# Where the operands of TensorE's products lie in SBUF, modulo 256 bytes

## The reference

```python
h = rmsnorm(x, norm_g[i, 0]); proj = h @ w_in[i]    # 9216 columns, split in seven parts
y_a = rg_lru(conv(rnn_in)) * gelu(rnn_gate); y_b = diff_attention(q, k, v)
merged = sigmoid(g_a) * (y_a @ w_proj_a[i]) + sigmoid(g_b) * (y_b @ w_proj_b[i])
x = x + rmsnorm(merged @ w_out[i], norm_g[i, 1])
h = rmsnorm(x, norm_g[i, 2])
f = swiglu(h, ffn_w_gate, ffn_w_up, ffn_w_down)    # layer 0, inner width 3584
f = sum over top-2 of 8 experts of combine * swiglu(h, w_gate[e], w_up[e], w_down[e])   # layer 1
x = x + rmsnorm(f, norm_g[i, 3])
gate = sigmoid(rmsnorm(x, norm_g[i, 4]) @ ple_w_gate[i])
x = x + rmsnorm(gate * (p[i] @ ple_w_proj[i]), norm_g[i, 5])
```

## Time and profile before

| | before |
|---|---|
| median of 3 runs | 1839.1 us (1839.0 to 1843.63) |
| profiled execution | 1839.69 us |
| its span, first to last instruction | 1838.0 us |
| TensorE busy | 1794.3 us, 98% |
| VectorE busy | 1490.0 us, 81% |
| ScalarE busy | 1302.3 us, 71% |
| read from HBM and written | 503.87 MB and 7.88 MB, 278 GB/s over the span |

### The profile page before, as it was taken

The page is one execution under the profiler, slowest core; times in us unless marked ns, Lnnn a source line. Parts: engine busy times, 40 slices in busy tenths (PEclk is TensorE's granted clock), DMA queues, the critical chain, the costliest instruction groups (busy, mean ns, idle before and its releaser), DMA issues.

```text
span 1838.0 us, 29753 instructions
## 1 busy us (share of the span) xinstructions
PE 1794.3 (98%) x10521; PEld 1568.4 (85%) x10521; DVE 1490.0 (81%) x1948; ACT 1302.3 (71%) x1726; POOL 112.3 (6%) x138
## 2 busy tenths in 40 slices
PE   6999999999999999999999999999999999999997
PEld 6998999999879999977888888888888888888785
DVE  7887667666468886668989989989899898998996
ACT  6757547454477657467878888788887887888776
POOL 1200000000010200002000000010000100000300
PEclk8999999999999999999999999999999999999999
DMA  9663555565545744567999999999999999999991
GB/s 308 206 186 124 174 195 185 187 203 194 197 146 174 221 151 140 197 191 254 396 378 380 376 373 387 368 384 366 382 387 370 381 385 369 384 372 374 390 370 49
DMA packets 276048, 517.01 MB, mean 281 GB/s; under 512 B 10754, under 2 KB 114052, under 8 KB 275972
## 3 DMA queue, kind: packets, MB, share of 16 engines
q1 hardware_dynamic: 268400, 493.81, 75.8%
q0 software_dynamic: 7248, 22.06, 3.7%
q10 hardware_dynamic: 324, 0.12, 0.0%
HBM read 503.87 MB, written 7.88 MB: 278 GB/s over the span
## 4 chain that ended last, share of the span: by engine, by line
PE 86%; DVE 6%; ACT 6%; issue 1%; DMA 0%; DVEq 0%; SPq 0%; ACTq 0%
PE bank L1759 81%; DVE wlo L1106 3%; ACT whi L647 1%; PE bank L2216 1%; PE bank L1914 1%; ACT SC L823 1%; ACT SQJ L658 1%; DVE RIN L1213 1%; DVE SC L1241 1%; ACT SC L818 0%; DVE X L1166 0%; PE bank L1870 0%; ACT HH L705 0%; PE bank L2226 0%; PE bank L1797 0%
## 5 line engine op out<-in xcount | busy, mean ns | idle before, releaser
L1106 DVE TENSOR_TENSOR wlo<-raw,whi 128x1024 fp32r<-128x1024 f32 x880 | 1031.6, 1223 | 157.6 <-ACT whi L647 153.8
L647 ACT ACTIVATE whi<-raw 128x1024 fp32r<-128x1024 f32 x880 | 919.4, 1059 | 317.7 <-PE bank L1759 308.9
L1759 PE MATMUL bank<-HH,whi 128*128 128x256 f32 x1296 | 364.5, 281 | 0.0
L1759 PE MATMUL bank<-HL,whi 128*128 128x256 f32 x1296 | 360.6, 278 | 0.0
L1759 PE MATMUL bank<-HH,wlo 128*128 128x256 f32 x1296 | 360.6, 278 | 0.0
L1759 PE MATMUL bank<-whi,XGH 128*128 128x512 f32 x896 | 358.1, 400 | 2.0 <-DVE wlo L1106 1.9
L1759 PE MATMUL bank<-whi,XGL 128*128 128x512 f32 x896 | 352.0, 393 | 0.0
L1759 PE MATMUL bank<-wlo,XGH 128*128 128x512 f32 x896 | 348.6, 389 | 0.0
L1759 PEld LDWEIGHTS bank<-HH,wlo 128*128 128x128 f32 x1296 | 244.8, 189 | 0.0
L1759 PEld LDWEIGHTS bank<-HH,whi 128*128 128x128 f32 x1296 | 243.6, 188 | 0.9 <-issue 0.7
L1759 PEld LDWEIGHTS bank<-HL,whi 128*128 128x128 f32 x1296 | 244.1, 188 | 0.2
(11 more groups left out here) (349 smaller groups left out, 2083.8 us busy)
## 6 DMA issues: line engine op xcount, KB each, us to landing
raw<-in_moe_w_gate_dram SPq DMA_DIRECT2D x112, 1024.0 KB, 7.1
raw<-in_moe_w_up_dram SPq DMA_DIRECT2D x112, 1024.0 KB, 7.6
raw<-in_moe_w_down_dram SPq DMA_DIRECT2D x112, 1024.0 KB, 6.0
raw<-in_w_in_dram SPq DMA_DIRECT2D x56, 1024.0 KB, 5.8
raw<-in_ffn_w_gate_dram SPq DMA_DIRECT2D x14, 1024.0 KB, 5.1
raw<-in_ffn_w_up_dram SPq DMA_DIRECT2D x14, 1024.0 KB, 5.0
raw<-in_ffn_w_down_dram SPq DMA_DIRECT2D x14, 1024.0 KB, 5.0
raw<-in_w_proj_a_dram SPq DMA_DIRECT2D x8, 1024.0 KB, 5.1
```

Source lines behind the costliest of these rows:

```text
L647: nc.scalar.activation(whi[b % SPL][:, r], raw[b % RAW][:, r], ACT.Copy).then_inc(s_hi, 1)
L1106: v.tensor_tensor(wlo[b % SPL][:, r], raw[b % RAW][:, r], whi[b % SPL][:, r].bitcast(F32), ALU.subtract).then_inc(s_lo, 1)
L1759: ins = mm(dst, a, b, start=start and n == 0, stop=stop and n == 2, skip_group_check=True)
```

## The change

The instructions are the same, in the same order and with the same waits on all five engines; their addresses change. SGN, of which only the first column was ever used, is cut from 128 columns to one, which frees 480 bytes. A helper `beside(off, phase)` rounds an offset up to the next one that lies `phase` bytes behind the first weight slot, modulo 256 (`LANE`). `arena` is rounded to 192 (`MOVING`), and `a1`, 16 KB behind it, to 0 (`HELD`). The block diagonal tile BD lies 8 KB + 256 behind `o_rin` rather than 8 KB + 128, and YAL and all later tiles of the mixer's part with it. The dense layer's second tiles (FH, FL, FS, FA) and the experts' (XGH, XGL, ATH, ATL, MS) are counted from `a1`.

```diff
+LANE = 256
+MOVING, HELD = 192, 0
...
         raw = [keep(f"raw{i}", [P, CH]) for i in range(RAW)]
+        first = cursor[0]
         whi = [keep(f"whi{i}", [P, CH], F32R) for i in range(SPL)]
...
-        SGN = keep("SGN", [P, P])
+        SGN = keep("SGN", [P, 1])
...
-        arena = cursor[0]
+
+        def beside(off, phase):
+
+            return off + (first + phase - off) % LANE
+
+        arena = beside(cursor[0], MOVING)
...
         o_rin = a0 + 16 * KB
+        a1 = beside(o_rin, HELD)
         RIN = at("RIN", o_rin, [P, KT, SEQ + 3])
-        o_bd = o_rin + 8 * KB + 128
+        o_bd = o_rin + 8 * KB + LANE
         BD = at("BD", o_bd, [P, 2, KT, P])
         YAH = at("YAH", o_rin, [P, KT, SEQ], F32R)
         YAL = at("YAL", o_bd, [P, KT, SEQ], F32R)
...
-        FH = at("FH", a0 + 16 * KB, [P, FT, SEQ], F32R)
-        FL = at("FL", a0 + 44 * KB, [P, FT, SEQ], F32R)
-        FS = at("FS", a0 + 72 * KB, [P, 2, 512])
-        FA = at("FA", a0 + 76 * KB, [P, 2, 512])
+        FH = at("FH", a1, [P, FT, SEQ], F32R)
+        FL = at("FL", a1 + 28 * KB, [P, FT, SEQ], F32R)
+        FS = at("FS", a1 + 56 * KB, [P, 2, 512])
+        FA = at("FA", a1 + 60 * KB, [P, 2, 512])
...
-        XGH = at("XGH", a0 + 16 * KB, [P, KT, TOKENS], F32R)
-        XGL = at("XGL", a0 + 20 * KB, [P, KT, TOKENS], F32R)
-        ATH = at("ATH", a0 + 24 * KB, [P, FT, TOKENS], F32R)
-        ATL = at("ATL", a0 + 38 * KB, [P, FT, TOKENS], F32R)
+        XGH = at("XGH", a1, [P, KT, TOKENS], F32R)
+        XGL = at("XGL", a1 + 4 * KB, [P, KT, TOKENS], F32R)
+        ATH = at("ATH", a1 + 8 * KB, [P, FT, TOKENS], F32R)
+        ATL = at("ATL", a1 + 22 * KB, [P, FT, TOKENS], F32R)
...
-        MS = at("MS", a0 + 52 * KB, [P, 2, 512])
+        MS = at("MS", a1 + 36 * KB, [P, 2, 512])
```

More of the change, by code:

```diff
@@ L161, in bass_hybrid_rglru_diffattn_moe @@
         PLO = at("PLO", o_rt + 14 * KB, [P, PKT, SEQ], F32R)
-        GROW = (at("GROW0", o_q, [P, D]), at("GROW1", a0 + 72 * KB, [P, D]), at("GROW2", o_q + 8 * KB, [P, D]),
+        GROW = (at("GROW0", o_q, [P, D]), at("GROW1", a1 + 56 * KB, [P, D]), at("GROW2", o_q + 8 * KB, [P, D]),
                 at("GROW3", o_q, [P, D]), at("GROW4", a0 + 12 * KB, [P, D]), at("GROW5", o_q + 8 * KB, [P, D]))
-        ZG = (at("ZG0", o_q + 4 * KB, [P, D]), at("ZG1", a0 + 76 * KB, [P, D]), at("ZG2", o_q + 12 * KB, [P, D]),
+        ZG = (at("ZG0", o_q + 4 * KB, [P, D]), at("ZG1", a1 + 60 * KB, [P, D]), at("ZG2", o_q + 12 * KB, [P, D]),
               at("ZG3", o_q + 4 * KB, [P, D]), at("ZG4", a0 + 52 * KB, [P, D]), at("ZG5", o_q + 12 * KB, [P, D]))
@@ L204, in bass_hybrid_rglru_diffattn_moe @@
         PLACE = at("PLACE", o_l + 512, [P, 5, BLK, EXPERTS])
-        assert a0 + 56 * KB <= o_q
+        assert a1 + 40 * KB <= o_q
         PT = at("PT", o_rt, [P, DEPTH * BLK, PLE])
@@ L491, in _ @@
             pool.memset(IDENT[:, :], 0.0).then_inc(s_pool, 1)
-            pool.memset(SGN[:, 0:1], 1.0).then_inc(s_sgn, 1)
+            pool.memset(SGN[:, :], 1.0).then_inc(s_sgn, 1)
             pool.memset(ONES[:, :], 1.0).then_inc(s_pool, 1)
@@ L508, in _ @@
                 pool.wait_ge(s_sgn, n + 1)
-                pool.affine_select(out=SGN[:, 0:1], in_=SGN[:, 0:1], compare_op=ALU.is_ge, fill=fill, base=-row,
+                pool.affine_select(out=SGN[:, :], in_=SGN[:, :], compare_op=ALU.is_ge, fill=fill, base=-row,
                                    pattern=[[0, 1]], channel_multiplier=1).then_inc(s_sgn, 1)
```

## The result

The changed kernel takes 1829.74 us (median of 6 runs, 1829.12 to 1831.46); the kernel before, run beside it, takes 1841.13 (6 runs, 1837.74 to 1843.63). The ratio is 0.9939, with a 95% interval of 0.9926 to 0.9952: faster by 0.6%. Predicted were 1817 us, within 1785 to 1842. The sign held, and so did the mechanism, that placement alone changes TensorE's step; of the 22 us forecast about half came. The six runs of the kernel before lie in two groups (1837.7 to 1839.1 and 1843.2 to 1843.6), so the difference of the medians, 11.4 us, can be anything from 9 to 14 us by the interval. The stages are compared in the two profiled executions. The profiled execution took 1829.26 us, its span 1827.6 against 1838.0, so 10.4 us are to be placed.

What follows compares the result with a forecast made beforehand. TensorE, busy in 98% of the 1838.0 us span, was taken as the bound, so time is matmuls times step. Terms of -19.2 and -2.8 made -22 us, from 1839.7 to 1817.7, said as 1817 us, range 1785 to 1842.

Steps and rivals of the forecast that it cites:

- YAH, YAL, PHI, PLO: Projections and embedding: with YAL, PHI, PLO moved from 64 to 192, steps fall by about 4.4 ns; sum -2.8 us.
- The fear that the first projection would fall into the higher level: First projection might step like the five mixer chunks at 117.8 ns, leaving -1.1 us instead of -2.8.
- HH, HL at nothing: Mixer and dense chunks: placement stays at 192, so no change entered; level shifts could cost 6 us or give 10.
- XGH to FL: Experts and dense down: 4368 matmuls with held operand moved from 192 to 0, 228.9 to 224.5 ns each, -19.2 us.
- f32 row: Comparison step for 512-column products: 228.9 and 233.3 ns were said to carry surcharge over it, so something was left to lose.
- Rival 1: Experts and dense down: two levels fall, to 1797 us, or three up to VectorE's cap, to about 1788; chance 0.23.
- What would hide a gain: Experts: VectorE caps the gain at 44 us, and transfers need 383 GB/s; a limit there would take 17.7 us.
- More than one level: Experts and dense down: the step falls by two levels (1797 us) or three (about 1788 us); chance 0.23.
- Held distance doesn't matter: Products with held state: the moving operand's place alone decides, leaving 0 to -3 us, 1836 us; chance 0.24, shared with a DMA limit.
- DMAs cap the experts: Experts: landings grow late from 377 GB/s on, leaving 0 to -3 us, 1836 us; chance 0.24, shared with held distance not mattering.
- Its remark that levels also come from elsewhere: Support for held distance not mattering: HH shows two levels at one placement, so levels can come from elsewhere; chance 0.24.
- Distance 0 collides: Experts and dense down: both operands' reads meet at once, step rises to 233.3 ns, +19.2 - 2.8, 1856 us; chance 0.19.

Runs made afterwards that it cites:

- e1: Changed kernel with the held tiles (FH, FL, XGH, XGL, ATH, ATL) back at distance 192, low parts still moved: 1835.46 us, ratio 0.9976 to the kernel before.
- e2: Changed kernel with YAL, PHI, PLO and all tiles behind BD back at 64, held tiles still at 0: 1829.56 us, ratio 0.9943 to the kernel before.
- e3: Changed kernel with HELD at 64 instead of 0: 1854.93 us, ratio 1.0077 to the kernel before.
- e5: Changed kernel with the tiles behind BD and YAL (T2 to SGA, MA, PHI, PLO) back at 64, YAL at 192: 1830.72 us, ratio 0.995 to the kernel before.
- m3: TensorE alone, no part of the reference: six placements, each entered twelve ways behind transposes or f32 products; moving at 192 gave 113.3 ns in 9 entries, 117.8 in 3.
- m1: TensorE alone, no part of the reference: the changed kernel's products with state tiles at eight distances and more; steps 226.7 to 234.2 ns held, 113.3 to 120.0 moving.
- e7: Changed kernel with the mixers' low weights at distance 128 instead of 0, except in the V chunks: 1825.02 us, ratio 0.9923 to the kernel before.
- m2: TensorE alone, no part of the reference: low parts of state and weights each at 0, 64, 128 or 192; state held at 0 gave 226.7 to 233.5 ns.
- e4: Changed kernel with MOVING at 0 instead of 192, so every arena tile is at 0: 1846.81 us, ratio 1.0034 to the kernel before.

## Why the prediction was half right

*YAH, YAL, PHI, PLO: right.* Predicted -2.8 us; the products priced give about 2.5 (1.18 and 1.16 in the projections' stages, some 0.15 for PHI and PLO). That the stages add up to 2.8 is chance in its last 0.3: 0.34 of the 0.38 us in the second embedding's stage lies in the gathering of the first expert's tokens (5.73 to 5.39 us), which the prediction doesn't price. First projection 21.76 us (21.8 predicted), output projection's 48 in 10.98 (10.99). e1 and e2 show that this is the place of YAL and the tiles behind it: it comes with them alone and goes with them. The fear that the first projection would fall into the higher level did not come true: with YAL at 192 the projections' stage is 67.3 us in both layers of the changed kernel, e1, e3 and e5.

*HH, HL at nothing: right, but for 1 us.* Chunks changed level in both directions, 44 of 86 low before and 49 after, which is 1.0 us in the two mixers; dense gate and up didn't move. The open question "what chooses between 113.3 and 117.8" has its answer in m3: both are steady states of one placement, and what runs just ahead chooses. The address of HH itself has no part at the distances tried (m1, 256 and 448). e7 shows it the other way round: with the low weights at 128 the choice is gone where the weights are held.

*XGH to FL: this step failed, by its size.* It said: "I take one level down, 228.9 - 4.4 = 224.5 ns", with "one level is the smallest amount in which steps have moved" as a reason. The 4.4 ns between the mixer's chunks and the dense ones are the distance of two states of one placement (m3), and no size of what a placement gives. Nor are the steps a ladder of 4.4 ns: m1 has 226.7, 228.9, 233.3 and 234.2 on the held side, 113.3, 116.7, 117.3, 117.8, 118.3 and 120.0 on the moving side. What distance 0 gives is 2.2 ns, 4368 x 2.2 = 9.7 us instead of 19.2. That the step would fall at all was not derived either: no row had both operands at 0, and m1's 233.3 at most other distances shows how near the other side was. So the sign of this term was in part luck.

No run shows the 224.5 ns: the lowest step at 512 columns is 226.7 (m1, m2, m3). Nor does one show that the "f32 row", with which the same sentence compares, is a measure for it. That row is 215.4 ns, (1.89 - 0.382)/7 from the earlier trace rows, and it is the step of one record: the 32 f32 products of U and BD that the kernel issues have 64 records, and the 120 of 256 columns in m3 (L97) have 240. Such a product takes two steps, 431 ns, where an fp32r product of 256 columns takes 113.3. That one of these records is the work of 512 fp32r columns was the author's estimate. Rival 1's 13.5 ns for the dense matmuls, behind the 1788 us of the range, are 228.9 less these 215.4, and no run shows them either: 2.2 ns came. The 215 and 108 ns of the rivals in m1 and m2 stand near the same row and its half; 226.7 and 113.3 are the lowest steps there.

*What was left out: the settling.* Of those 9.7 us, about 6.5 arrived: 0.62 in dense down's 288 matmuls, 8 times 0.74 in the experts. (The stages give 1.27 and 5.19, the same sum by chance: 0.65 of it lies behind dense down, in work that the change doesn't price, and the last expert's gate and up took 0.31 us more than before rather than less, with TensorE's waits for `wlo` there at 1.0 us instead of 0.6.) TensorE's timeline of the changed kernel in the fourth expert, behind transposes of MA:

```profile
1322.16 0.60 PE L2225 MATMUL bank<-IDENT,MA 128*128 128x128 f32 x4
1322.52 0.48 PE L1768 MATMUL bank<-whi,XGH 128*128 128x512 f32 x1
1322.83 0.40 PE L1768 MATMUL bank<-wlo,XGH 128*128 128x512 f32 x1
...
1324.46 0.40 PE L1768 MATMUL bank<-whi,XGL 128*128 128x512 f32 x1
```

and at the same place in the kernel before:

```profile
1330.67 0.60 PE L2216 MATMUL bank<-IDENT,MA 128*128 128x128 f32 x4
1331.03 0.48 PE L1759 MATMUL bank<-whi,XGH 128*128 128x512 f32 x1
...
1332.95 0.39 PE L1759 MATMUL bank<-whi,XGL 128*128 128x512 f32 x1
```

Eight steps take 1.94 us after (1322.52 to 1324.46) and 1.92 before, though the steady step is shorter after. An expert has nine such interruptions, seven by MA and two by XROW. The first 16 steps behind MA's take 3761 ns (median) in both kernels, so the 35 ns that 16 shorter steps should give are missing. From behind one interruption to behind the next, 48 products and 4 transposes, after and before:

```profile
1107.80:1119.18 11.38, 11.38 (x55) 9.40 (x54) 10.37 (x11) 9.36 (x11) 0.00 (x0) 1.00 1.05 387
1114.97:1126.42 11.45, 11.45 (x55) 9.41 (x54) 10.37 (x11) 9.35 (x11) 0.00 (x0) 1.00 1.05 387
```

That is 0.07 us less, where 48 x 2.2 ns are 0.11. So each interruption takes back 0.04 us, nine of them 0.37: 504 x 2.2 = 1.11 less 0.37 is 0.74, as measured. Over eight experts that is 3.0 us, and 9.7 - 3.0 = 6.7. m3 shows the same sign with TensorE alone. The rows before held a hint: two experts take 238.95 us between equal starts, 0.45 more than the 238.5 added up from steady steps and transposes.

*What would hide a gain: right that it doesn't.* In the changed kernel's experts two to seven TensorE keeps to its steps, with VectorE at 90%; only in the first and the last expert does it wait for `wlo`, 0.6 and 1.0 us in all (1.4 and 0.6 before).

*The rivals.* More than one level: fell, no placement of m1 or m2 at 512 columns is under 226.7 ns. Held distance doesn't matter: fell by e3 and m1. DMAs cap the experts: fell by the changed kernel's own, which run at 226.7 ns with 380 GB/s. Its remark that levels also come from elsewhere was true: one placement can have two. Distance 0 collides: fell for the products of 512 columns that it was about. But those of 256 columns stand at 120.0 ns there, the highest level of m1's row, with the state moving or held (e4, m2). The 233.3 ns that this rival named are a real step too: e3 runs near it, and m1 has 234.2 at distance 96.

*Open.* Why these distances act as they do. The best are 0 at 512 columns and 192 at 256, and the low parts count too (m2); no rule was found that gives both. Why MA's place alters its transposes and the products behind them (118.74 against 118.51) was seen, not explained.

## What to carry to other kernels

Where TensorE is busy all the time, read its step from start times, and if equal products have unequal steps, look at operands' offsets modulo 256 bytes: here products of 512 and of 256 columns want different distances, and the low parts count too. A dozen placements with TensorE alone cost one run and would have given this change's steady step at once; a level seen elsewhere in the trace doesn't give it. Enter each placement in several ways, since one look can show one of two states. Where products are interrupted every few microseconds, measure the steps behind the interruption as well as the steady one.

## What the runs showed of the hardware

- A three-term fp32r product of 512 columns steps by 226.7 to 234.2 ns, one of 256 columns by 113.3 to 120.0, by where its operands lie modulo 256 bytes, with no other engine at work (m1). Distance 0 is the lowest at 512 columns (226.7, m1). At 256 columns it stands at the highest level of m1's row with the state moving (120.0, as do 96 and one run at 128), and at 120.0 against 117.8 at 192 with the state held (m2); in e4 both sides stand at 120.0. In the full kernel that is 1829.7 us against 1854.9 (e3) and 1846.8 (e4).
- One sequence of products on one set of addresses has two steady steps, 113.3 and 117.8 ns, that last for the whole run of 48 (m3) or of several chunks (28.27 us in the mixer), and are chosen by what ran just ahead. At 512 columns with the state held at 192 it is 228.9 ns in 11 entries of 12 and 233.3 in one (m3).
- Behind transposes the 512-column products need 81 to 129 ns more than steady steps would, most of it in the first (m3), and the placement with the shorter steady step has the longer settling (95 to 129 ns at 0 against 81 to 106 at 192).
